# Attention scores as three products of rounded queries and keys, and not as one fp32 product

## What is computed

```python
qkv = h @ w_qkv
q = q.reshape(B, S, H, dh).astype(jnp.float32) * (dh ** -0.5)
...
s_own = jnp.einsum('bchd,bshd->bchs', qc, k_own)
s_own = s_own - slopes[None, None, :, None] * dist_own.astype(jnp.float32)[None, :, None, :]
s_own = jnp.where((dist_own >= 0)[None, :, None, :], s_own, NEG)
...
p = jax.nn.softmax(scores, axis=-1)
```

## Time and profile before

| | |
|---|---|
| median of 3 runs | 876.56 us |
| the profiled execution's own time | 876.48 us |
| its span, first to last instruction | 874.4 us |
| PE busy | 866.7 us, 99% |
| DVE busy | 643.6 us, 74% |
| ACT busy | 463.8 us, 53% |
| granted PE clock | 1.00 of 2.4 GHz in all but the last slices |

### The profile page before, as it was taken

How to read it: one execution, slowest core, us unless ns; L and a number is a source line. 1 busy time by engine, 2 the same in 40 slices (tenths; PEclk the granted TensorE clock), 3 DMA queues, 4 the chain that set the end, 5 groups by cost and what they waited for, 6 DMA issues and landing times.

```text
span 874.4 us, 12503 instructions
## 1 busy us (share of the span) xinstructions
PE 866.7 (99%) x5231; PEld 763.8 (87%) x5231; DVE 643.6 (74%) x752; ACT 463.8 (53%) x542; POOL 22.7 (3%) x49
## 2 busy tenths in 40 slices
PE   9999999999999999999999999999999999999997
PEld 7888888889999988888888888888888988888885
DVE  6998776568777699777655697777656998777452
ACT  6765555434555665555534375555544665555441
POOL 1000006200000000000000000000000000000000
PEclk9999999999999999999999999999999999999999
DMA  7777655665444447665556566555565377565431
GB/s 239 247 248 231 193 181 171 194 209 161 146 145 145 145 145 241 193 193 181 179 184 196 175 193 197 192 190 182 179 191 171 99 240 235 187 213 182 150 115 48
DMA packets 154535, 159.69 MB, mean 183 GB/s; under 512 B 3000, under 2 KB 152816, under 8 KB 154480
## 3 DMA queue, kind: packets, MB, share of 16 engines
q1 hardware_dynamic: 154128, 158.35, 56.6%
q10 hardware_dynamic: 352, 0.55, 0.2%
HBM read 157.84 MB, written 1.05 MB: 182 GB/s over the span
## 4 chain that ended last, share of the span: by engine, by line
PE 99%; DVE 0%; ACT 0%; issue 0%; POOL 0%; DVEq 0%; POOLq 0%; ACTq 0%
PE psum L444 97%; PE psum L760 1%; PE psum L743 1%; PE psum L642 0%; PE psum L634 0%; PE psum L474 0%; ACT soft L937 0%; DVE band L1208 0%; DVE scratch L1251 0%; DVE scratch L1220 0%; POOL ident L407 0%; PE psum L646 0%; POOL ident L406 0%; DVEq L87 0%; DVE rstd L1115 0%
## 5 line engine op out<-in xcount | busy, mean ns | idle before, releaser
L444 PE MATMUL psum<-xg,w_hi 128*128 128x512 f32 (+1 forms) x1664 | 490.5, 379 | 0.1
L1068 DVE TENSOR_TENSOR w_lo<-raw,w_hi 128x2048 fp32r<-128x2048 f32 (+1 forms) x148 | 330.1, 2231 | 109.7 <-ACT w_hi L841 109.7
L444 PEld LDWEIGHTS psum<-xg,w_lo 128*128 128x128 f32 x1536 | 289.2, 188 | 62.6
L841 ACT ACTIVATE w_hi<-raw 128x2048 fp32r<-128x2048 f32 x149 | 277.6, 1867 | 113.5 <-PE psum L444 112.0
L444 PE MATMUL psum<-xg,w_lo 128*128 128x256 f32 x1536 | 312.9, 278 | 0.0
L444 PEld LDWEIGHTS psum<-xg,w_hi 128*128 128x128 f32 x1664 | 254.6, 189 | 1.8 <-issue 0.7
L444 PE MATMUL psum<-h_all,w_hi 128*128 128x512 f32 (+1 forms) x656 | 189.4, 374 | 0.0
L444 PEld LDWEIGHTS psum<-h_all,w_lo 128*128 128x128 f32 x592 | 111.4, 188 | 23.4
L444 PE MATMUL psum<-h_all,w_lo 128*128 128x256 f32 x592 | 121.8, 278 | 0.0
L444 PEld LDWEIGHTS psum<-h_all,w_hi 128*128 128x128 f32 x656 | 100.2, 189 | 0.8 <-issue 0.8
L878 ACT ACTIVATE scratch<-psum 128x512 f32<-128x512 f32 x44 | 26.1, 593 | 79.5 <-PE psum L444 79.5
(11 more groups left out here) (114 smaller groups left out, 484.2 us busy)
## 6 DMA issues: line engine op xcount, KB each, us to landing
raw<-in_ffn_w_gate_dram SPq DMA_DIRECT2D x42, 1024.0 KB, 5.3
raw<-in_ffn_w_up_dram SPq DMA_DIRECT2D x42, 1024.0 KB, 5.3
raw<-in_ffn_w_down_dram SPq DMA_DIRECT2D x24, 1024.0 KB, 5.1
raw<-in_attn_w_qkv_dram SPq DMA_DIRECT2D x12, 1024.0 KB, 5.1
raw<-in_ffn_w_down_dram SPq DMA_DIRECT2D x20, 512.0 KB, 4.3
raw<-in_ffn_w_down_dram SPq DMA_DIRECT2D x12, 768.0 KB, 4.3
raw<-in_attn_w_o_dram SPq DMA_DIRECT2D x4, 1024.0 KB, 5.0
raw<-in_ffn_w_gate_dram SPq DMA_DIRECT2D x7, 256.0 KB, 6.0
```

Source lines behind the costliest of these rows:

```text
L444: return nc.tensor.matmul(out, stationary, moving, start=start, stop=stop, skip_group_check=True)
L841: nc.scalar.activation(w_hi[:, n % SPL, 0:size], raw[:, n % RAW, 0:size], ACT.Copy).then_inc(hi_split, 1)
L1068: nc.vector.tensor_tensor(w_lo[:, n % SPL, 0:size], raw[:, n % RAW, 0:size], w_hi[:, n % SPL, 0:size].bitcast(f32), ALU.subtract).then_inc ...
```

## The change

Queries and keys are split as the weights are. After `qkv_scale`, ACT rounds them into `h_all` (`round_qk`), DVE writes the rest beside it (`rest_qk`), and each score matmul becomes three in fp32r. The PE now waits for `qk_lo_done`, which the subtraction of k signals, and no longer for the scaled k. The chunks of `h_all` that are written (8 to 11) are not used elsewhere in this stage. The split q and k have one buffer, not two.

```diff
+        qk_parts = [[h_all[:, DC + GM * s:DC + GM * (s + 1), part, :] for s in range(2)] for part in range(2)]
...
                 if half == 0:
-                    pe.wait_ge(qkv_scaled, 3 * j + 2)
+                    pe.wait_ge(qk_lo_done, 2 * (j + 1))
...
-                    for hh in heads:
-                        last = mm(bank(head_bank(j, hh))[:, cols], q_sb[head_rows(hh), j % 2, half, q],
-                                                k_sb[head_rows(hh), j % 2, half, keys], start=True, stop=True)
+                    for part, (q_part, k_part) in enumerate(((0, 0), (0, 1), (1, 0))):
+                        for hh in heads:
+                            last = mm(bank(head_bank(j, hh))[:, cols], qk_parts[q_part][0][head_rows(hh), half, q],
+                                      qk_parts[k_part][1][head_rows(hh), half, keys], start=(part == 0),
+                                      stop=(part == 2))
...
+            def round_qk(j, s):
+                act.wait_ge(qkv_scaled, 3 * j + s + 1)
+                nc.scalar.activation(qk_parts[0][s], (q_sb, k_sb)[s][:, j % 2], ACT.Copy).then_inc(qk_hi_done, 1)
+
+            round_qk(0, 0)
+            round_qk(0, 1)
             split_hi(ATT0 + SPL)
             split_hi(ATT0 + 1 + SPL)
...
-                    split_hi(ATT0 + 3 * j + 2 + SPL)
-                    split_hi(ATT0 + 3 * j + 3 + SPL)
+                    for s in range(2):
+                        split_hi(ATT0 + 3 * j + 2 + s + SPL)
+                        round_qk(j + 1, s)
...
+            def rest_qk(j, s):
+                dve.wait_ge(qk_hi_done, 2 * j + s + 1)
+                nc.vector.tensor_tensor(qk_parts[1][s], (q_sb, k_sb)[s][:, j % 2], qk_parts[0][s].bitcast(f32),
+                                        ALU.subtract).then_inc(qk_lo_done, 1)
...
             qkv_scale(0, 0)
             qkv_scale(0, 1)
+            rest_qk(0, 0)
+            rest_qk(0, 1)
             split_lo(ATT0 + SPL)
...
                     for s in range(2):
                         split_lo(ATT0 + 3 * j + 2 + s + SPL)
+                        if s:
+                            rest_qk(j + 1, 0)
                         qkv_scale(j + 1, s)
...
                 split_lo(ATT0 + 3 * j + 4 + SPL)
                 if j < QUADS - 1:
+                    rest_qk(j + 1, 1)
                     qkv_scale(j + 1, 2)
```

More of the change, by code:

```diff
@@ L225, in build_trunk @@
         qkv_scaled = sem("qkv_scaled")
+        qk_hi_done = sem("qk_hi_done")
+        qk_lo_done = sem("qk_lo_done")
         score_done = sem("score_done")
```

## The result

The changed kernel takes 894.05 us, the median of four runs (892.79 to 894.77), against 876.70 us of the kernel before beside it, a ratio of 1.0196 with a 95% interval from 1.0184 to 1.0209. It is 17.35 us slower; forecast were 17.8, and a range of 890.0 to 899.2. The profiled execution took 892.79 us, the lowest of the four, so its trace accounts for 16.4 us of span and not for all of the median.

A forecast was written before the change was run, and what follows sets the result against it. The prediction took the PE to bound the kernel, with added waits stalling it: 876.5 + 14.9 (the ACT and DVE string) + 2.9 (half clock after gaps) = 894.3 us, range 890 to 899.2.

The forecast's parts named there:

- The bound: Whole kernel: PE busy 866.7 of 874.4 us, so only PE work or waits that stop the PE change the time.
- The score block: PE scores per full quad: 24 matmuls in 12 slots take 1.45 us instead of 1.51, -0.06 per quad.
- Rival 3: Score block: fp32r products with 64 rows don't run side by side, +1.39 us per quad, +2.9 in all; chance 0.08.
- The string: Attention stage: ACT and DVE steps follow by turns, 17.77 us from ACT's first round of weights to the next scores.
- second gap: PE before quad 1's scores, after the values of quad 0: a wait of 4.0 us.
- Rival 4: Attention stage: ACT and DVE absorb the added work, only the score block counts, 876.3 us, not slower; chance 0.05.
- The clock: After each of three PE gaps: 2.75 us at half speed, 1.4 us of work lost; +2.9 us in all.
- size in quad 3: Quad 3 at half clock: all of the 1.4 us of lost work is passed on.
- +2.9: Half clock after the gaps: 0.75 us passed on in each of quads 1 and 2, 1.4 in quad 3.
- 14.9 us of the string: Attention stage: lateness of 6.53 us from quad 0 plus 4.20 us each from quads 1 and 2.
- Rivals 1: Attention stage: stalls of 4 us, but the clock stays at 1.00, 891.4 us; chance 0.25.
- 2 (898.4): Attention stage: stalls, and half clock for as long as at the start, +7.0 us, 898.4 us; chance 0.12.

The follow-up runs named there:

- e1_both: Changed kernel with ACT's roundings of q and k behind the probability copies and DVE's rests ahead of the third weight split: 877.03 us, ratio 1.0008.
- e8_same: The changed kernel once more, nothing altered, for a second trace: 893.63 us, ratio 1.0200 to the kernel before; its profiled execution took 896.55 us.
- e4_fp32: Changed kernel with fp32 score products again, keeping its roundings, subtractions and waits: 892.06 us, ratio 1.0177 to the kernel before.
- e9_fill_last: Changed kernel with 26 spare fp32r products on the PE ahead of the scores of quad 3 alone: 891.82 us, ratio 1.0173 to the kernel before.
- e10_packed: e1_both with two narrow products merged into one of 256 columns, plus one DVE addition per head: 876.12 us, ratio 0.9994 to the kernel before.
- e2_act: Changed kernel with only ACT's order changed, roundings of q and k behind the probability copies: 882.58 us, ratio 1.0067 to the kernel before.

## Why the prediction came out, point by point

- **The bound.** Right: the PE sets the time, and waits of the PE are what was added; with them gone (e1_both) the time is the old one.
- **The score block.** 12 slots, heads side by side: from 211.23 to 212.80 it is 1.57 us, where 1.45 was forecast and 1.51 stood before. So +0.06 per quad, not -0.06. Rival 3 falls: 24 products one after the other would be 2.90. A narrow product is hardly cheaper than a wide one, as the forecast assumed: 0.112 us from start to start on average against 0.117 for 256 columns. What the forecast lacked is the first wide product behind the narrow ones, twice per block: 0.17 us to the next start.
- **The string.** Right to 0.02 us: 17.79, 17.79 and 17.78 us from ACT's first round to the next scores, against 17.77. Quad 0 cost 6.53 us as forecast. Its second gap is 2.67 and not 4.0 us, because half clock stretched the values ahead of it (2.82 us, not 1.45) into the same room. In the same way the gap before quad 2's scores is 2.50, and the PE idles 11.4 us in the stage where about 15 were forecast; the lateness is the same. Quads 1 and 2 cost 4.11 and 4.12, forecast 4.20: the old period began with ACT 8.15 us after the scores, and it is 8.04 now. Rival 4, that the engines absorb the work, falls in the written order and holds in that of e1_both.
- **The clock: the step that was wrong.** I wrote "ACT's first round of weights needs the q tile used, at about 7.5 us after the scores", with 0.65 us of slack and 0.75 passed on in quads 1 and 2. It needs the tile four places earlier. That is the v tile of the same quad, used before the scores even start; the q tile releases ACT's second round. In quad 1 half clock stretched the q and k tiles from 11.61 to 12.97 us, and ACT's first round still came 8.04 us after the scores (239.50 to 247.54). Nothing was passed on: 25.83 us with half clock and 25.83 without. Only what half clock takes from the score block itself is passed on, for ACT's exponentials hang on it: 0.13 us in quad 1 of e8_same, and 0.44 in that of e4_fp32, where the whole block ran at half clock.
- **And the size in quad 3.** There all of it is passed on, as I wrote, but it is more than 1.4: 1.5 us in the first trace, 2.9 in e8_same (3.41 and 6.83 us at half clock). The executions without a trace tell only their mean granted clock, not where it fell: the first trace has 0.993, that of e8_same 0.990, and of the six other runs of the changed kernel three have 0.990, two 0.992 and one 0.993. With 2.9 the sum is 876.6 + 14.8 + 0.1 (the score blocks of quad 3) + 2.9 = 894.4 us, with 1.5 it is 893.0; the two medians, 894.05 and 893.63, lie between. That fits, but no run shows what quad 3 took in them. The forecast's +2.9 thus came out near by luck: it is 0.75 + 0.75 + 1.4, where the traces have 0 to 0.1, 0, and 1.5 to 2.9. The 14.9 us of the string are not luck, since each quad came as forecast. Rivals 1 (891.4) and 2 (898.4) both fall: the first is what e9_fill_last makes true by force.
- **Left open.** The scores of quad 0 start between 210.9 and 213.4 us in the traces of all kernels here. Part of that is when a weight tile lands early in the kernel, as e8_same shows, and the spread is as large as the clock's term. So the last microsecond of the median's 17.35 is not assigned. Nor do the runs show why a low stretch lasts 3.41 us in one execution and 6.83 in another.

## What to carry to other kernels

When an in-order engine gets a helper instruction that waits for another engine, write down both engines' instructions by turns and add up from start to start; busy shares of 53 and 74% hid a string of 17.8 us in which the two engines stand in turn. Put the helper behind everything that others wait for and that doesn't need it, and ahead of everything that its own reader doesn't need: four moved calls give back all but 0.5 of the 17.4 us. To price a clock fall, follow who waits for the stretched work; where a wait of another engine ends later anyway, it costs nothing, and it costs where that engine itself waits for the stretched work, here the score block.

## What the runs showed of the hardware

- An fp32r matmul with 128 moving columns and 64 rows takes 0.112 us from start to start per pair of heads, on average over the six of a score block, almost what 256 columns take (0.117); one product of 256 columns in the place of two of 128 saved 0.2 us of a block of 1.57 (e10_packed).
- The Trainium skill, "TensorE: Matmul & The Clock Gate", section "LDWEIGHTS (loading the stationary operand)", gives the time of a load in ns as its columns divided by 1.2, whatever its rows: about 107 for 128 columns, an estimate from that formula. The 0.112 us is near it; no run here separates the load from the product.
- Two heads on the lower and the upper 64 rows overlap in fp32r as in fp32: the two start 3 or 4 ns apart in the trace after, and 24 products take 1.57 us.
- PE gaps of like length do not always bring the clock down: it fell behind the gap of 2.29 us in e2_act, not behind the 2.50 us before quad 2's scores in the first trace of the changed kernel, yet behind the same gap (2.58 us) in e8_same. The low stretches in the stage lasted 3.41 or 6.83 us.
- Half clock costs less than it takes from the PE where the PE waits anyway: of about 4.8 us of lost work (the estimate above) 1.5 came through in the first trace.
